# Seven block products in place of eight in the feed-forward up projections of a three-layer float32 network

## The reference

```
h2 = rms_norm(x, gain)
x  = x + jnp.square(jax.nn.relu(h2 @ w_ff_up)) @ w_ff_down     # 1024 -> 4096 -> 1024
```

## Time and profile before

| | |
|---|---|
| three runs | 2377.58, 2378.5, 2379.65 us; median 2378.5 |
| span of the profiled execution (first to last instruction) | 2376.0 us |
| granted TensorE clock, mean | 1.00 |
| TensorE busy | 2350.2 us, 99% of the span |
| weight loads busy | 1918.1 us, 81% |
| VectorE busy | 1330.4 us, 56% |
| ScalarE busy | 936.5 us, 39% |
| GpSimd busy | 156.3 us, 7% |

### The profile page before, as it was taken

How to read it: one execution, slowest core, us unless ns; L and a number is a source line. 1 busy time by engine, 2 the same in 40 slices (tenths; PEclk the granted TensorE clock), 3 DMA queues, 4 the chain that set the end, 5 groups by cost and what they waited for, 6 DMA issues and landing times.

```text
span 2376.0 us, 32832 instructions
## 1 busy us (share of the span) xinstructions
PE 2350.2 (99%) x12976; PEld 1918.1 (81%) x12976; DVE 1330.4 (56%) x1963; ACT 936.5 (39%) x1475; POOL 156.3 (7%) x196
## 2 busy tenths in 40 slices
PE   8999999999999999999999999999999999999999
PEld 6877778787888888877678888888888888888887
DVE  7656556778553443567764334356755557533433
ACT  5444464457242332446553223243423224422321
POOL 5111110000002200012220000000000000000000
PEclk9999999999999999999999999999999999999999
DMA  4222223222333323321033233322222212333322
GB/s 161 71 72 69 66 61 109 73 71 81 98 96 111 104 88 96 106 62 54 27 98 106 89 98 106 88 89 89 77 66 81 88 57 80 120 89 99 99 88 78
DMA packets 60639, 205.80 MB, mean 87 GB/s; under 512 B 7249, under 2 KB 7249, under 8 KB 60386
## 3 DMA queue, kind: packets, MB, share of 16 engines
q1 hardware_dynamic: 59760, 202.93, 28.5%
q10 hardware_dynamic: 754, 1.14, 0.2%
HBM read 201.94 MB, written 2.10 MB: 86 GB/s over the span
## 4 chain that ended last, share of the span: by engine, by line
PE 94%; DVE 3%; ACT 1%; issue 1%; POOL 1%; DMA 0%; SPq 0%; DVEq 0%; ACTq 0%
PE psum L1724 84%; PE psum L1785 1%; PE psum L1887 1%; PE psum L1751 1%; PE psum L1858 1%; PE psum L1792 1%; PE psum L1840 1%; PE psum L1881 1%; POOL arena L597 1%; PE psum L1802 0%; PE psum L1798 0%; PE psum L1760 0%; PE psum L1830 0%; DVE arena L1325 0%; DVE cols L1331 0%
## 5 line engine op out<-in xcount | busy, mean ns | idle before, releaser
L1724 PE MATMUL psum<-hhi,whi 128*128 128x512 f32 x1640 | 646.3, 394 | 10.4 <-DVE wlo L1048 8.4
L1724 PE MATMUL psum<-hlo,whi 128*128 128x512 f32 x1640 | 643.9, 393 | 0.0
L1724 PE MATMUL psum<-hhi,wlo 128*128 128x512 f32 x1640 | 642.0, 391 | 0.0
L1724 PE MATMUL psum<-uhi,whi 128*128 128x512 f32 x1392 | 545.7, 392 | 0.0
L1724 PE MATMUL psum<-ulo,whi 128*128 128x512 f32 x1392 | 544.1, 391 | 0.0
L1724 PE MATMUL psum<-uhi,wlo 128*128 128x512 f32 x1392 | 542.9, 390 | 0.0
L1048 DVE TENSOR_TENSOR wlo<-raw,whi 128x1024 fp32r<-128x1024 f32 (+1 forms) x399 | 466.8, 1170 | 57.0 <-ACT whi L1010 31.6
L1724 PEld LDWEIGHTS psum<-hhi,whi 128*128 128x128 f32 x1640 | 308.4, 188 | 76.1 <-issue 12.1
L1724 PEld LDWEIGHTS psum<-hhi,wlo 128*128 128x128 f32 x1640 | 308.4, 188 | 64.3 <-issue 0.2
L1724 PEld LDWEIGHTS psum<-hlo,whi 128*128 128x128 f32 x1640 | 308.7, 188 | 61.7 <-issue 0.2
L1010 ACT CAST whi<-raw 128x1024 fp32r<-128x1024 f32 x190 | 199.6, 1051 | 351.9 <-PE psum L1724 351.9
(11 more groups left out here) (251 smaller groups left out, 1758.4 us busy)
## 6 DMA issues: line engine op xcount, KB each, us to landing
raw<-in_packed_dram SPq DMA_DIRECT2D x359, 512.0 KB, 3.6
raw<-in_packed_dram SPq DMA_DIRECT2D x40, 256.0 KB, 2.6
x<-in_xt_dram SPq DMA_DIRECT2D x8, 256.0 KB, 5.5
out_dram<-x SPq DMA_DIRECT2D x8, 256.0 KB, 2.0
arena<-in_near_bias_dram ACTq DMA_DIRECT2D x1, 1024.0 KB, 6.1
vec<-in_vec_dram ACTq DMA_DIRECT2D x1, 44.0 KB, 4.1
arena<-in_gla_gate_up_dram ACTq DMA_DIRECT2D x1, 32.0 KB
arena<-in_gla_gate_bias_dram ACTq DMA_DIRECT2D x1, 2.0 KB
```

The lines of the kernel that those rows point to most:

```text
L1724: mm = pe.matmul(g, w[:, u % 4, k, :], v[:, k, :], start=n == 0, stop=n == 3 * kt - 1)
```

## The change

Two consecutive up units, output tiles j and j+4, become a pair. Seen as a 2 x 2 block product (input features halved, positions halved), the pair needs eight products of four input tiles by 256 positions. The changed kernel makes seven, by Strassen's scheme in Winograd's form. Each is 12 matmuls of 128 x 256, so a pair has 84 of those in place of 48 of 128 x 512, and each goes to its own PSUM bank.

- The activations' four blocks and four sums of them, high and low halves, are made once for each feed-forward part, beside the last units of the stage before (`normed_hi`, `normed_lo`, `sums_high`, `sums_low`).
- Four sums of weight blocks for each pair are made on GpSimd (`weight_sums`: four operations of 128 x 512). One of them is written over `raw`, before ScalarE rounds it; three go to `w_diff` (128 x 1536), which ScalarE rounds (`diff_high`) and VectorE completes (`diff_low`).
- The outputs are put together from the seven banks: ScalarE copies three (`copy_product`), VectorE adds four (`add_product`, `last_sum`), and two sums follow on GpSimd (`first_row_joined`, `second_row_joined`; on VectorE for the last pair of a block). Then relu times `rstd` runs from SBUF (`rectify`), and square, rounding and low half as before.
- `HALVED` gives the order 0, 4, 1, 5, 2, 6, 3, 7 to up units, to the tiles a down unit takes in, and to the last eight units ahead of each feed-forward part. The loops are unrolled.

The core of the diff, first the lists of the pair on each engine:

```diff
+            def weight_sums(q):                                    # GpSimd
+                u = UP_AT[2 * q]
+                v = u + 1
+                for w in (u, v):
+                    pool.wait_ge(raw_in[w % 4], 16 * (w // 4 + 1))
+                if q:
+                    pool.wait_ge(diff_lo_done, q)
...
+                pool.tensor_tensor(s3, a11, a21, ALU.subtract).then_inc(w_sums, 1)
+                pool.wait_ge(w_sums, 4 * q + 1)
+                pool.tensor_tensor(a21, a21, a22, ALU.add).then_inc(w_sums, 1)
+                pool.wait_ge(w_sums, 4 * q + 2)
+                pool.tensor_tensor(s2, a21, a11, ALU.subtract).then_inc(w_sums, 1)
+                pool.wait_ge(w_sums, 4 * q + 3)
+                pool.tensor_tensor(s4, a12, s2, ALU.subtract).then_inc(w_sums, 1)
+            def up_stage(i):
+                for q in range(16 * i, 16 * i + 16):
+                    if q < 16 * i + 15:
+                        weight_sums(q + 1)
+                    if q % 4 < 3:
+                        first_row_joined(pool, q)
+                        second_row_joined(pool, q)
+            def up_pair(u, n):                                     # ScalarE
+                q = pair_of(u)
+                j = q % 4
+                if j:
+                    continue_with(u - 2)
+                split_hi(u + 2)
+                copy_product(q, 1, 1, 0)
+                if j:
+                    continue_with(u - 1)
+                copy_product(q, 2, 1, 1)
+                copy_product(q, 3, 0, 0)
+                if n is not None:
+                    norm(n)
+                split_hi(u + 3)
+                if j < 3:
+                    diff_high(q + 1)
+            def last_sum(q):                                       # VectorE
+                dve.wait_ge(up_added, 4 * q + 3)
+                if q:
+                    dve.wait_ge(up_joined, 2 * q)
+                add_product(q, up_mid[1], up_mid[0], 6)
+            def up_pair(u, n):
+                q = pair_of(u)
+                j = q % 4
+                s = up_out[q % 2][:, 0, :]
+                if j:
+                    last_sum(q - 1)
+                    post(u - 2)
+                split_lo(u + 2)
+                if j:
+                    rectify(u - 1)
+                split_lo(u + 3)
+                if j:
+                    post(u - 1)
...
+                add_product(q, up_mid[0], s[:, 0:HALF_T], 4, 3)
+                dve.wait_ge(up_added, 4 * q + 1)
+                add_product(q, s[:, 0:HALF_T], s[:, 0:HALF_T], 0)
+                if j < 3:
+                    diff_low(q + 1)
+                add_product(q, s[:, HALF_T:SEQ], up_mid[0], 5)
+                if n is not None:
+                    dve.wait_ge(norm_rstd, n + 1)
+                if j == 3:
+                    first_row_joined(dve, q)
+                rectify(u)
+            def up_pair(u, n):                                     # TensorE
+                q = pair_of(u)
+                first_four = ((0, 0, B21), (1, 1, T4), (2, 2, T1), (3, 3, B11))
+                def before(order):
+                    if order == 0:
+                        pe.wait_ge(lo_done, u + 1)
+                        if q % 4 == 0:
+                            pe.wait_ge(posted, u if (u - 1) % 2 == 0 else u - 1)
+                        if q:
+                            pe.wait_ge(up_added, 4 * q - 2)
...
+                    if order == 2:
+                        pe.wait_ge(lo_done, u + 2)
+                    if 1 <= order <= 3 and q:
+                        pe.wait_ge(up_copied, 3 * q - 3 + order)
+                    if order == 4:
+                        pe.wait_ge(diff_lo_done, q + 1)
+                        if q:
+                            pe.wait_ge(up_added, 4 * q - 3)
+                    if order >= 5 and q:
+                        pe.wait_ge(up_added, 4 * q - 6 + order)
```

Then the first unit after the pairs, and the norm's operands:

```diff
+                    for j in range(KD):                            # VectorE, down units
+                        u = b + 16 * f + KD + j
+                        if j == 0:
+                            last_sum(pair_of(u - 1))
+                            second_row_joined(dve, pair_of(u - 1))
+                            rectify(u - 1)
+                            post(u - 2)
+                        if u + 2 < len(units):
+                            split_lo(u + 2, kt=units[u + 2][4])
...
+                        post(u - 1)
+                if n in FFNORMS:                                   # VectorE, normed_lo, for every second tile
...
+                    dve.tensor_tensor(t1, b12, b11, ALU.subtract).then_inc(h_sums, 1)
+                    dve.tensor_tensor(t3, b22, b12, ALU.subtract).then_inc(h_sums, 1)
...
+                    dve.tensor_tensor(t2, b22, t1, ALU.subtract).then_inc(h_sums, 1)
...
+                    dve.tensor_tensor(t4, b21, t2, ALU.subtract).then_inc(h_sums, 1)
```

More of the change, by code:

```diff
@@ L91, in ff @@
         for f in range(FB):
-            for j in range(KD):
+            for j in HALVED:
                 units.append(("up", w1, row, f * D + P * j, KD, j))
@@ L155, in w_out_e @@
     def w_out_e(half):
-        return [("down", "w_out_e_2", 512 * half, P * j, 4, j) for j in range(KD)]
+        return [("down", "w_out_e_2", 512 * half, P * j, 4, j) for j in (HALVED if half else range(KD))]
     specs = [("head", w, 0, QA + P * i, KD, ("a", "q", i)) for i in range(4)]
@@ L187, in plan @@
                 [r[0], None, r[1], [r[2], r[3]], r[4], None, r[5], None])
-    todo += [(("down", "w_out_o_2", D + 4 * P, P * j, 4, j), None) for j in range(KD)]
+    todo += [(("down", "w_out_o_2", D + 4 * P, P * j, 4, j), None) for j in HALVED]
     pipeline("l3", todo)
@@ L530, in ff @@
             def ff(i):
-                with sp.Fori(0, FB) as f:
-                    for j in range(16):
-                        load(steps[f"ff{i}"] + j, f * 16, steps[f"ff{i}"] + j + f * 16)
+                for u in range(steps[f"ff{i}"], steps[f"ff{i}"] + 16 * FB):
+                    load(u)
             load(0)
@@ new lines, in copy_product @@
+            def copy_product(q, order, which, half):
+                act.wait_ge(product, 7 * q + order + 1)
+                if q >= 2:
+                    act.wait_ge(posted, UP_AT[2 * (q - 2) + which] + 1)
+                o = up_out[q % 2][:, which, HALF_T * half:HALF_T * half + HALF_T]
+                nc.scalar.copy(o, psum[:, order, 0:HALF_T]).then_inc(up_copied, 1)
+            def up_pair(u, n):
[14 more added lines that the diff above has]
+                    diff_high(q + 1)
@@ new lines, in add_product, with rectify @@
+            def add_product(q, o, src, order, copies=0):
+                dve.wait_ge(product, 7 * q + order + 1)
+                if copies:
+                    dve.wait_ge(up_copied, 3 * q + copies)
+                dve.tensor_tensor(o, src, psum[:, order, 0:HALF_T], ALU.add).then_inc(up_added, 1)
+            def rectify(u):
+                q, second = pair_of(u), UPU[u] % 2
+                s = up_out[q % 2][:, second, :]
+                if not second:
+                    dve.wait_ge(up_added, 4 * q + 2)
+                dve.wait_ge(up_joined, 2 * q + 1 + second)
+                dve.scalar_tensor_tensor(out=s, in0=s, scalar=0.0, in1=rstd, op0=ALU.max, op1=ALU.mult).then_inc(evacuated, 1)
```

364 lines of the change are left out of this document (249 added, 115 removed).

## The result

| | before | after |
|---|---|---|
| four runs, median (lowest to highest) | 2378.04 (2377.51 to 2379.65) us | 2607.79 (2606.26 to 2608.7) us |
| ratio, 95% interval | | 1.0963 (1.0948 to 1.0979): slower |
| span of the profiled execution | 2376.0 us | 2605.4 us |
| granted TensorE clock, mean | 1.00 | 0.963 |

What follows compares the result with a forecast made beforehand. The chain through the engines' lists with turns between GpSimd and VectorE, 15.0 us a middle pair, was to bound it, not TensorE. Span 2376.0 + 146 (blocks) + 18 (norm's operands) = 2540, time 2542 us, range 2485 to 2605.

Steps and rivals of the forecast that it cites:

- the chain of a pair in the middle of a block: From one pair's first `rectify` to the next pair's, through three engines' lists: 13.15 us, against 9.8 of TensorE.
- the last pair's 11.2: Last pair of a block, without `diff_low` or weight sums beside it and joined on VectorE: 11.2 us.
- GpSimd and VectorE at once: Middle pairs: both engines take turns where both read two SBUF operands, lengthening 13.15 us to 14.85 or 15.3; 15.0 taken.
- rival 1: Turns at the port are hidden in VectorE's waits: 13.15 us a pair, 2498 us in all; chance 15%.
- A 256-position matmul: TensorE's part in a pair: 0.117 us each, 84 of them 9.8 us.
- Rivals 2 and 3: First: TensorE stays the bound, 2354 us, 4%. Second: 256-position matmuls cost 0.215 to 0.226 us, 2790 us, 4%.
- Rival 2: TensorE stays the bound in the up units, a block then 45.4 us; 2354 us in all; chance 4%.
- The norm's operands: Ahead of feed-forward parts VectorE's extra sums and low halves come late: +18 us, from 5 to 35.
- The clock: Idle TensorE may fall to half clock, some 2 us lost; charged nothing since 9.8 + 2 stays under 15 a pair.
- Rival 4: The lower clock falls on the chain in every pair, 48 x 2 = +96 us: 2640 us; chance 6%.
- A block: Up units to the end of the first down unit: 61.1 us against 48.9 before, +146 us over twelve blocks.
- The own range's edge of 2585: Upper end of the main forecast's own range, 2515 to 2585 us (14.3 to 15.8 a pair, norm 5 to 35); chance 69%.

Runs made afterwards that it cites:

- kernel 1: The changed kernel with the weight sums on GpSimd at 16 of 512 columns, the rest of the sums left out; 2534.82 us.
- kernel 3: The changed kernel with `split_hi(u+3)` moved ahead of the second row's square in ScalarE's list, same work; 2544.85 us.
- kernel 6: The changed kernel with weight sums at 16 columns and the steps from PSUM copies to low half at 32, the rest left out; 2378.94 us.
- kernel 4: The changed kernel with the first weight sums of a part one tile of the norm earlier in GpSimd's list; 2603.21 us.
- kernel 7: The changed kernel with the operands' four sums at 32 of 256 columns and their halves taken of another block; 2596.48 us.
- kernels 8 and 9: First: the changed kernel with its lists in another order, all sums kept, 2481.14 us. Second: that with weight sums at 16 of 512 columns, 2386.83 us.
- kernel 9: The reordered kernel with all sums kept (2481.14 us), its four weight sums then cut to 16 of 512 columns; 2386.83 us.

## Why the forecast's mechanism held, and which step failed

**What bounds the change** was read rightly: the chain through the lists, not TensorE. The term "the chain of a pair in the middle of a block", 13.15 us, is 13.22 in kernel 1; the last pair's 11.2 is 11.17; kernel 3 shows the wait for `split_hi(u+3)` as one of its links, since the last pairs get 2.6 us shorter without it.

**GpSimd and VectorE at once.** Of the two layouts worked out, 14.85 if VectorE goes first and 15.3 if GpSimd does, the second holds: 15.26. At 712.2 GpSimd's L689, which had stood ready since 711.24, goes ahead of `rectify`. The 2.04 us between it and kernel 1 are this step, and rival 1 (turns hidden) falls. The Trainium skill (SBUF — State Buffer, SBUF: two separate sides) states that the port pair of the two is a lock, held for a whole instruction by the one that starts first. The trace agrees, with the split at 2.20 us, and the runs show besides that with both lists full the two alternate.

**A 256-position matmul** was put at 0.117 us: 0.118 here, 9.83 for 84 in kernel 6. One number of its working does not come out of the rows: two matmuls of 128 positions at 0.11 make 0.22, so a 512 has some 0.004 over them and not 0.013. With that the value would be 0.115, so the sum does not hang on it. Rivals 2 and 3 fall. Rival 2's block of 45.4 us, which it named as the price if TensorE stayed the bound, is 45.9 in kernel 6.

**The step that failed is "The norm's operands"**, the +18 us with an upper end of 35: it measured 52. The forecast added VectorE's operations into 5.4 us of a turn and took what exceeds it, "some 2 us late for each two tiles". It did not follow three things: the one buffer that ScalarE and VectorE hand to and fro (ScalarE waits 3.42 us for the sums), the first weight sums, which either make ScalarE wait (4.26 us) or collide with VectorE (kernel 4), and the operands of the last tiles as a chain that runs on into the first pair. That last part is 23.7 us in the three first blocks, against 2 in the forecast for `ff0` and nothing for the others; 10 of it go with the size of the weight sums (kernel 1). The four sums themselves, which the forecast did count, are 3 us of the 14 ahead of each part (kernel 7). The walk from list to list that was made for the pair was not made here.

**The clock** was charged nothing, with the reason that 2 us fit into a pair. For pairs that holds: middle pairs take 15.24 to 15.28 us throughout, those that start at the lower clock too. But a fall can also come where TensorE is the bound, behind a block's last idle time: ten falls, 16 us in all. Rival 4 had the right size for a fall (2 us, measured 1.6) and the wrong place.

**A block** was 61.1 and is 62.55: 0.4 in the first pair, 0.5 in the middle ones (15.0 was a middle between 14.85 and 15.3), and 0.4 in the tail, with up to 0.7 more where a fall of the clock reaches into it. Times twelve, 17 us, of which some 2 are the clock's.

So of the 65 us by which the forecast's 2540 us of span fell short, 34 are the norm's operands, 16 the clock and 15 the blocks. The own range's edge of 2585 left 43 for all of them, with 17 for the norm and nothing for the clock. That the time lies only 2.8 us above 2605 is no merit of the range: its upper end was there for rival 4, whose mechanism, a lower clock on the chain of every pair, did not happen.

**Not settled.** How the first blocks' 23.7 us and the 11 us that kernel 7 leaves ahead of a part divide between the handing over, the wider operations and the waits for weight sums; a second `h_parts` buffer was not tried. What decides whether the clock falls behind an idle time of 2.4 us is open too: nine blocks have the fall and three do not, among them the third of `ff0`, whose pairs and idle time are like those of its neighbours.

## What to carry to other kernels

Fewer operations on the engine that bounds a kernel are worth only what the other engines' lists can follow: write down the order of each list and walk from one instruction to the same one a period later, before counting work. Do that for the transitions too, where a buffer changes hands for each tile, and not for the steady part alone. Work given to an idle GpSimd is paid for by a busy VectorE where both read two operands from SBUF, one wait for each operation: kernels 8 and 9 differ by 94 us, and only in the width of the weight sums.

## What the runs showed of the hardware

- With both lists full, VectorE and GpSimd alternate by operation, not by time: 0.69 us become 1.77 or 1.80, a split of 1.22 becomes 2.20, and an addition of 1.30 on GpSimd 1.6 to 2.15 (after, kernel 3). Operations of VectorE with an input in PSUM keep their time: the additions L1821 of 256 positions take 0.41 or 0.42 beside an addition on GpSimd too, those to x (L1345) 0.68 or 0.69.
- An addition of 16 columns on GpSimd takes 0.22 us where VectorE has no operation of that kind (kernel 9), and 1.20 beside a split (kernel 1): it ends just after the split does, whose 1.23 stay.
- After the same idle time of 2.41 to 2.43 us, TensorE starts again once at the full clock, with its matmuls 0.43 apart only from 842.24 on, and once at the lower clock at once (1043.23). Either costs 1.6 us. Blocks alike in their pairs take 45.8 or 47.3 to 47.4 us of tail and down units within one execution.
- Matmuls of 256 positions, each with its own weight load, stand 0.117 to 0.118 us apart at the full clock and 0.21 at the lower one.
